# The state-space scan carried out inside the attention loop of a hybrid encoder layer

## The chip, the cores and the metric

The kernel runs on one core of a Trainium2 chip. The metric is the device time of one execution in microseconds (us), as the median of several runs. A profiled execution comes with its own time, with its span (from its first to its last instruction) and with the clock that was granted to TensorE.

## The reference, cut to what matters

One encoder layer on 1024 tokens of width 1024, all in float32:

```python
proj = x @ w_in                       # 512 columns u, 256 c_q, 128 + 32 ckv_rope
s = gelu(s5_bidirectional(u, ...))    # 32 groups of 16 channels, 64 complex states, two directions
s = s * sigmoid(s @ w_glu + b_glu)
a = mla(c_q, ckv_rope, ...)           # 8 heads, 1024 x 1024 scores each, softmax, times v
x1 = layer_norm(alpha * x + concat([s, a]) @ w_o)
out = layer_norm(alpha * x1 + moe(x1))  # 64 experts, top 6, one shared
```

`s5_bidirectional` runs, for each group and direction, the linear recurrence h[l] = a * h[l-1] + B u[l] over the 1024 tokens (backwards for the second direction) and reads it out as C h. `s` and `a` depend on `proj` alone and meet first in the product with `w_o`.

## The kernel before, in words

The stages stand one behind the other, each in a block of its own with a barrier at its end: `project` (projection, latents, coefficients of the scan), `attention`, `s5_scan`, `s5_gate`, `mix_norm_route`, `moe_experts`. Within a block each engine has its own list of instructions in a fixed order, written out by hand, and waits on counting semaphores for the others. `project` writes u to memory (`u_d`) and `s5_scan` reads it back from there; nothing of the scan depends on the attention.

`attention` (L480) loops over 8 heads, two to an iteration of the loop, and in a head over 8 tiles t of 128 queries. For a tile:

- TensorE multiplies queries by keys into `p_s` (`scores`, L529: two matmuls of 512 columns).
- VectorE takes the maximum of each row (`top`, L645) and scales it (L646). ScalarE takes the exponential into `pr` (L615), with the row's total beside it.
- TensorE transposes `pr` in eight blocks into `p_t` (L568). VectorE copies the first four blocks to `prT` (L659), ScalarE the last four (L620).
- TensorE multiplies `prT` by v into `p_o` (L582: eight matmuls). VectorE takes the reciprocal of the total (L650) and stores the scaled result (L651). These two are `finish`.

In the first seven tiles of a head TensorE also makes one of seven parts of the next head (`part`: two of q, L543; two of k, L546; two of turned q, L556; one of v, L550), which ScalarE copies out of the one bank `p_p` (`keep_part`). In tile 2 VectorE rotates the next head's q (`rotate`). `p_s`, `pr` and `prT` have two buffers each. In tile t TensorE's order is: wait for `pr` of tile t, transposes, scores of tile t + 2, the part, the product with v.

`s5_scan` (L684) works in 4 batches of 8 groups. For each of the two directions VectorE makes the matrices that bring the inputs of 8 tokens into the state (`combine` into `vs`, L867 to L869), the phases of the rotation (`tables`, L876 to L878), and the matrices that read the state out (`edges`: `ed1`, `ed2`). TensorE transposes `vs` (L766) and ScalarE copies the result to `w_in` (L807, L808). ScalarE makes sines and cosines of the phases (L811 to L814). TensorE multiplies `w_in` by the inputs U (`effects`, L752), and VectorE runs the recurrence on that (`run_states`, L847 to L859: rotate, scan, rotate back). TensorE also makes the short convolution within 8 tokens (L781). SyncE rearranges it from `ka` to `kt` by eight DMAs. At the end of a batch TensorE sums everything into `p_y` (L793 to L798), ScalarE copies it to `ysb` (L822), and SyncE stores it to `ys_d` by eight DMAs. U is loaded by eight DMAs at the start of the stage (L732). The eight PSUM banks are all in use, in either stage.

Of the kernel before, what the change touches and what calls it, by code (L numbers as in the profile page):

```python
# [13 lines left out]
P = 128  # L14
# [465 lines left out]
def attention(nc, k):  # L480
    SCALE = DQ ** -0.5
    with ExitStack() as ctx:
# [8 lines left out]
        bias = sb("bias", [P, 2], f32)  # L491
# [11 lines left out]
        scored, biased, probs, p_turned, pT_dve, pT_act = sem("scored"), sem("biased"), sem("probs"), sem("p_turned"), sem("pT_dve"), sem("pT_act")  # L503
        o_done, o_read, own = sem("o_done"), sem("o_read"), sem("own")
        PARTS = ("q", "q", "k", "k", "qT", "qT", "v")
        ROTATE = 2
        LINKS = 2 * T + 1
        block = ctx.enter_context(nc.Block())

        @block.sync  # L510
        def _(sp):
            def load(h, u):
                sp.dma_start(wq[:, u], k.w_uq[0].rearrange("(k p) n -> p k n", p=P)[:, :, bass.ds(h * DQ, DQ)]).then_inc(w_in[u], 16)
                sp.dma_start(wkv[:, u, :], k.w_ukv[0][:, bass.ds(h * (NOPE + DV), NOPE + DV)]).then_inc(w_in[u], 16)
            load(0, 0)
            load(1, 1)
            with sp.Fori(1, HEADS // 2) as hh:
                for u in range(2):
                    h = hh * 2 + u
                    sp.wait_ge(part_done, (h - 1) * len(PARTS))  # L520
                    load(h, u)

        @block.tensor
        def _(pe):
            def scores(h, u, t):
                if t == 0:
                    pe.wait_ge(part_kept, h * len(PARTS) + 6)
                for half in range(2):
                    last = nc.tensor.matmul(p_s[:, t % 2, half * 512:(half + 1) * 512], qT[:, u, t * P:(t + 1) * P],  # L529
# [3 lines left out]
            def part(h, u, i, nth_weights=None, first=False):  # L533
                what, second = PARTS[i], PARTS[:i].count(PARTS[i])
                if nth_weights is not None:
                    pe.wait_ge(w_in[u], nth_weights)
                if not first:
                    pe.wait_ge(part_kept, h * len(PARTS) + i)
# [19 lines left out]

            def head(hh, u, following):

                h = hh * 2 + u
                for t in range(T):
                    n = h * T + t
                    pe.wait_ge(probs, n + 1)
                    for half in range(2):
                        for r in range(4):
                            j = half * 4 + r
                            last = nc.tensor.transpose(p_t[:, j, :], pr[:, t % 2, j * P:(j + 1) * P], k.ident)  # L568
                        last.then_inc(p_turned, 1)
                    if t + 2 < T:  # L570
                        scores(h, u, t + 2)
                    elif following:
                        scores(h + 1, 1 - u, t + 2 - T)
                    if following and t < len(PARTS):
                        part(h + 1, 1 - u, t, (hh + u) * 32 + 32 if t == 0 else None)
                    pe.wait_ge(pT_dve, n + 1)
                    pe.wait_ge(pT_act, n + 1)
                    if t == 0:
                        pe.wait_ge(part_kept, h * len(PARTS) + 7)
                    pe.wait_ge(o_read, n + 1)  # L580
                    for j in range(T):
                        last = nc.tensor.matmul(p_o[:, 0:DV], prT[:, t % 2, j, :], v[:, u, j, :], start=(j == 0), stop=(j == T - 1))  # L582
                    last.then_inc(o_done, 1)

            for i in range(len(PARTS)):
                part(0, 0, i, 32 if i == 0 else None, first=(i == 0))
            scores(0, 0, 0)
            scores(0, 0, 1)
# [7 lines left out]
        def _(act):  # L596
            def keep_part(h, u, i):
                what, second = PARTS[i], PARTS[:i].count(PARTS[i])
                act.wait_ge(part_done, h * len(PARTS) + (i + 1))
# [6 lines left out]
                else:  # L606
                    last = nc.scalar.activation(qT[:, u, second * 512:(second + 1) * 512], p_p[0:DQ, :], ACT.Copy)
                last.then_inc(part_kept, 1)

            def head(hh, u, following):  # L610
                h = hh * 2 + u
                for t in range(T):
                    n = h * T + t
                    act.wait_ge(biased, n + 1)
                    nc.scalar.activation(pr[:, t % 2, :], p_s[:, t % 2, :], ACT.Exp, bias=bias[:, t % 2:t % 2 + 1], scale=SCALE,  # L615
                                         accum_out=total[:, t % 4:t % 4 + 1]).then_inc(probs, 1)
                    if following and t:
                        keep_part(h + 1, 1 - u, t - 1)
                    act.wait_ge(p_turned, 2 * n + 2)
                    nc.scalar.activation(prT[:, t % 2, 4:8, :], p_t[:, 4:8, :], ACT.Copy).then_inc(pT_act, 1)  # L620

            for i in range(len(PARTS)):
                keep_part(0, 0, i)
            with act.Fori(0, HEADS // 2 - 1) as hh:
# [6 lines left out]
        def _(dve):  # L631
            def rotate(ch, h):
                dve.wait_ge(part_kept, h * len(PARTS) + 2)
                q1, q2 = q[:, :, NOPE:NOPE + 16], q[:, :, NOPE + 16:DQ]
                nc.vector.tensor_tensor(rot[:, 0], q1, k.cos, ALU.mult)
                nc.vector.tensor_tensor(rot[:, 1], q2, k.sin, ALU.mult)
                nc.vector.tensor_tensor(rot[:, 2], q1, k.sin, ALU.mult)
                ch.link(nc.vector.tensor_tensor(rot[:, 3], q2, k.cos, ALU.mult))
                nc.vector.tensor_tensor(q1, rot[:, 0], rot[:, 1], ALU.subtract)
# [1217 lines left out]
```

## Time and profile before

| | |
|---|---|
| time, median of 3 runs | 1795.45 us (1794.26 to 1797.92) |
| time of the profiled execution | 1796.62 us |
| its span, granted clock | 1794.8 us, 0.927 |
| TensorE (PE) busy | 1566.9 us, 87% |
| VectorE (DVE) busy | 852.5 us, 47% |
| ScalarE (ACT) busy | 361.4 us, 20% |
| GpSimd (POOL) busy | 432.9 us, 24% |

Times of rows are in microseconds from the start of the span, those marked ns apart. PE is TensorE's matmuls and PEld its weight loads, which overlap them. A float32 matmul shows as two records. The granted clock is 1.00 at 2.4 GHz and 0.50 at 1.2 GHz. In a timeline the brackets at the end of a row give how long the engine was idle before it, and what ended that. "x8" says that eight instructions are merged in the row.

### The profile page before, as it was taken

To read this page: it belongs to the slowest core of one execution; us is meant where nothing else is said; L and a number is where in the kernel's file an instruction comes from. 1 tells how busy PE (TensorE), PEld (TensorE's weight loads), DVE (VectorE), ACT (ScalarE), POOL (GpSimd) and SP (SyncE) were. 2 spreads that over 40 slices of the span, in tenths; PEclk is the share of its full clock that TensorE was granted. 3 is DMA by queue.
4 is the path that set the end of the run, shared out by engine and by line. 5 is a ranking of instruction groups with operands and counts; after the bars stand their busy time and mean duration, and the time that the engine had idled before them with its cause. 6 is when DMAs were issued, how large, how long until landed. Compare 5 with 4: busy or idle time off the path is not lost. (4 is left out here: it accounts for less than half of the span.)

```text
span 1794.8 us, 18459 instructions
## 1 busy us (share of the span) xinstructions
PE 1566.9 (87%) x5878; PEld 894.7 (50%) x5878; DVE 852.5 (47%) x1618; ACT 361.4 (20%) x616; POOL 432.9 (24%) x444
## 2 busy tenths in 40 slices
PE   7989999999946565389999999999999999999990
PEld 4546777777735554235554444444444444444440
DVE  1462444444588888333886433333333333333335
ACT  1303443443433113111221001000000000000014
POOL 0000000000000000000244345555555555555530
PEclk9997999999967666689999999999999999999995
DMA  9010000000061101540005689999999999999956
GB/s 233 12 43 4 5 4 4 4 4 1 1 52 19 23 12 23 182 158 24 36 25 202 237 287 368 367 368 360 362 368 366 365 362 367 365 371 366 361 153 207
DMA packets 105149, 317.26 MB, mean 177 GB/s; under 512 B 38358, under 2 KB 55406, under 8 KB 80146
## 3 DMA queue, kind: packets, MB, share of 16 engines
q1 hardware_dynamic: 80546, 257.26, 39.1%
q0 software_dynamic: 23408, 59.45, 13.6%
q8 instruction: 23, 0.38, 0.1%
q10 hardware_dynamic: 1152, 0.00, 0.0%
q14 instruction: 20, 0.16, 0.0%
HBM read 271.73 MB, written 51.72 MB: 180 GB/s over the span
## 5 line engine op out<-in xcount | busy, mean ns | idle before, releaser
L1548 PE MATMUL moe_p_gu<-mixers_ring,moe_xgT 128*128 128x512 f32 x784 | 344.6, 592 | 0.0
L1679 DVE STREAM_TRANSPOSE moe_xgT<-moe_xg 128x1024 f32<-128x1024 f32 x65 | 132.1, 2032 | 417.7 <-DMA moe_xg<-x_d,moe_idx 417.7
L1494 POOL DMA_INDIRECT moe_xg<-x_d,moe_idx x260 | 263.6, 1014 | 116.1 <-issue 60.1
L1121 POOL DMA_INDIRECT slot_d<-all_entry,all_dest_i x48 | 48.0, 1001 | 928.4 <-DVE all_dest_i L1333 916.2
L1568 PE MATMUL moe_p_y<-mixers_ring,moe_hT 128*128 128x512 f32 x520 | 233.9, 592 | 0.9 <-DVE moe_hT L1690 0.9
L1548 PEld LDWEIGHTS moe_p_gu<-mixers_ring,moe_xgT 128*128 128x128 f32 x784 | 145.7, 191 | 164.5 <-issue 164.5
L1505 POOL DMA_INDIRECT sum_d<-moe_y,moe_idx x65 | 105.4, 1622 | 243.8 <-DMA sum_d<-moe_y,moe_idx 206.4
L1568 PEld LDWEIGHTS moe_p_y<-mixers_ring,moe_hT 128*128 128x128 f32 x520 | 98.7, 190 | 125.0 <-issue 123.9
L1616 ACT ACTIVATE moe_sig<-moe_p_gu 128x256 f32<-128x256 f32 x65 | 24.9, 383 | 582.0 <-PE moe_p_gu L1548 582.0
L582 PEld LDWEIGHTS att_p_o<-att_v,att_prT 128*128 128x128 f32 x1024 | 120.4, 192 | 19.5 <-issue 17.6
L582 PE MATMUL att_p_o<-att_v,att_prT 128*128 128x64 f32 x1024 | 123.7, 274 | 1.5 <-DVE att_prT L659 1.5
L529 PE MATMUL att_p_s<-latents_kT,att_qT 96*128 96x512 f32 x256 | 122.8, 603 | 0.0
L645 DVE TENSOR_REDUCE att_nmax<-att_p_s 128x1 f32<-128x1024 f32 x64 | 78.4, 1225 | 92.5 <-PE att_p_s L529 92.1
L1548 PE MATMUL moe_p_gu<-mixers_o,moe_xgT 128*128 128x512 f32 x256 | 113.9, 598 | 1.0
L752 PE MATMUL ssm_p_v<-ssm_U,ssm_w_in 128*128 x256 | 53.6, 399 | 46.6 <-DVE ssm_gsn L859 29.7
L752 PEld LDWEIGHTS ssm_p_v<-ssm_U,ssm_w_in 128*128 128x128 f32 x256 | 50.7, 305 | 50.8 <-DVE ssm_gsn L859 32.4
L1548 PEld LDWEIGHTS moe_p_gu<-mixers_o,moe_xgT 128*128 128x128 f32 x256 | 47.3, 190 | 57.2 <-issue 57.2
L615 ACT ACTIVATE att_pr<-att_p_s,att_bias 128x1024 f32<-128x1024 f32 x64 | 70.9, 1108 | 3.1 <-DVE att_bias L646 3.1
L568 PE MATMUL att_p_t<-all_const,att_pr 128*128 128x128 f32 x512 | 66.9, 274 | 0.4 <-ACT att_pr L615 0.4
L620 ACT ACTIVATE att_prT<-att_p_t 128x512 f32<-128x512 f32 x64 | 38.2, 597 | 138.6 <-PE att_p_t L568 138.6
L1622 ACT ACTIVATE moe_y<-moe_p_y,shared_block_w 128x512 f32<-128x512 f32 x65 | 44.7, 688 | 100.7 <-PE moe_p_y L1568 97.9
L1696 DVE TENSOR_SCALAR moe_y<-moe_p_y,shared_block_w 128x512 f32<-128x512 f32 x65 | 48.7, 750 | 29.8 <-PE moe_p_y L1568 26.0
(314 smaller groups left out, 1968.1 us busy)
## 6 DMA issues: line engine op xcount, KB each, us to landing
mixers_ring<-in_we_down_dram SPq DMA_DIRECT2D x65, 1024.0 KB
mixers_ring<-in_we_gate_dram SPq DMA_DIRECT2D x49, 1024.0 KB
mixers_ring<-in_we_up_dram SPq DMA_DIRECT2D x49, 1024.0 KB
mixers_o<-in_we_gate_dram SPq DMA_DIRECT2D x16, 1024.0 KB
mixers_o<-in_we_up_dram SPq DMA_DIRECT2D x16, 1024.0 KB
moe_xg<-x_d,moe_idx POOLq DMA_INDIRECT x260
all_x_sb<-in_x_dram SPq DMA_DIRECT2D x8, 512.0 KB, 11.7
mixers_ring<-in_w_o_dram SPq DMA_DIRECT2D x1, 4096.0 KB, 22.2
```

Of the source, the lines that this page charges most:

```text
L529: last = nc.tensor.matmul(p_s[:, t % 2, half * 512:(half + 1) * 512], qT[:, u, t * P:(t + 1) * P], kT[:, u, half * 512:(half + 1) * 512], ...
L568: last = nc.tensor.transpose(p_t[:, j, :], pr[:, t % 2, j * P:(j + 1) * P], k.ident)
L582: last = nc.tensor.matmul(p_o[:, 0:DV], prT[:, t % 2, j, :], v[:, u, j, :], start=(j == 0), stop=(j == T - 1))
L615: nc.scalar.activation(pr[:, t % 2, :], p_s[:, t % 2, :], ACT.Exp, bias=bias[:, t % 2:t % 2 + 1], scale=SCALE, accum_out=total[:, t % 4:t ...
L645: ch.link(nc.vector.tensor_reduce(nmax[:, t % 2:t % 2 + 1], p_s[:, t % 2, :], AX.X, ALU.max, negate=True))
L752: last = nc.tensor.matmul(p_v[:, x % 2, part, r, :], w_in[:, gd, part * N:part * N + P], U[:, bass.ds(b * GB + half * 4 + r, 1), :].rearra ...
L1494: nc.gpsimd.indirect_dma_start(xg[:, u, g, :], None, x1_quarters, bass.IndirectOffsetOnAxis(ap=idx[:, c, g:g + 1], axis=0), bounds_check=N ...
L1505: nc.gpsimd.indirect_dma_start(k.sum_d[:, :], bass.IndirectOffsetOnAxis(ap=idx[:, c, NQ:NQ + 1], axis=0), y[:, u, :], None, compute_op=ALU ...
L1548: last = nc.tensor.matmul(p_gu[:, u, :], xgT[:, u, kk, :], k.moe_gu[v][:, :, kk * F:(kk + 1) * F], start=(kk == 0), stop=(kk == KD - 1))
L1568: last = nc.tensor.matmul(p_y[:, half * 512:(half + 1) * 512], hT[:, u, kk, :], k.moe_dn[v][:, kk * D + half * 512:kk * D + (half + 1) * 512],
L1679: nc.vector.transpose(xgT[:, u].rearrange("p k (g i) -> p g k i", g=NQ), xg[:, u].rearrange("p g (j k) -> p g k j", k=KD)).then_inc(x_turn ...
L1696: nc.vector.tensor_scalar(y[:, u, 512:D], p_y[:, 512:D], k.block_w[:, bass.ds(col, 1)], None, ALU.mult).then_inc(y_dve, 1)
```

## The change

`attention` and `s5_scan` become one block, `attend_and_scan`. The scan now goes in 8 batches of 4 groups, one batch per head, and each of its pieces has a fixed place in one of the 8 tiles of a head:

- VectorE does a piece of the scan in tiles 0 to 6, behind its copy of `p_t` and ahead of `finish`. All its operations on a batch have half the elements that they had, and there are twice as many batches.
- TensorE's transposes of `vs`, its kernels and its outputs stand behind the product with v (tiles 1 and 2; 3 and 4; 7), its effects ahead of it (tiles 3 and 5). Transposes, kernels and outputs share the bank `p_p` with the parts of the next head.
- ScalarE keeps `vs` turned, makes the sines and cosines of both directions in tile 2 (one Abs and two Sin of 128 x 1024 for each head), and keeps kernels and outputs.
- To make room, `p_s`, `pr` and `prT` go from two buffers to one. The scores of tile t + 1 now stand at the start of tile t, ahead of the transposes. ScalarE's exponential of tile t + 1 now stands behind its copy of `p_t` and behind `keep_part` of tile t.
- The scaling of the row maximum (L646) is gone: the scale goes into the copy of the turned q.
- U is loaded at the start of the combined block, and TensorE waits for it before the first head. The transfers of `kt` and `ys_d` stand in SyncE's list behind the loads of the weights of the head after next.
- The turned probabilities are copied half by VectorE, half by ScalarE, as before.

The core of the diff (bodies that only moved are left out; in round brackets what stands there unchanged):

```diff
-def attention(nc, k):
+def attend_and_scan(nc, k):
...
-        pr = sb("pr", [P, 2, SEQ], f32)
-        prT = sb("prT", [P, 2, T, P], f32)
-        p_s = ps("p_s", [P, 2, SEQ])
+        pr = sb("pr", [P, SEQ], f32)
+        prT = sb("prT", [P, T, P], f32)
+        p_s = ps("p_s", [P, SEQ])
+        p_v = ps("p_v", [P, 2, GB, NC])
+        quarters = p_p[:, :].rearrange("p (r n) -> p r n", r=GB)
...
# TensorE, head(): order within tile t
                     pe.wait_ge(probs, n + 1)
+                    if t + 1 < T:
+                        scores(h, u, t + 1)
+                    elif following:
+                        scores(h + 1, 1 - u, 0)
                     (eight transposes of pr into p_t)
-                    if t + 2 < T:
-                        scores(h, u, t + 2)
...
                         part(h + 1, 1 - u, t)
+                    if t == 3:
+                        effects(h, 0)
+                    if t == 5:
+                        effects(h, 1)
                     pe.wait_ge(pT_dve, n + 1)
                     pe.wait_ge(pT_act, n + 1)
...
                     (eight matmuls into p_o)
+                    if t in (1, 2):
+                        turn_vs(h, t - 1)
+                    if t in (3, 4):
+                        kernels(h, 4 - t)
+                    if t == 7:
+                        outputs(h)
...
+            pe.wait_ge(u_in, 16 * T)      # ahead of the first head
# ScalarE, head()
+                    act.wait_ge(p_turned, 2 * n + 2)
+                    nc.scalar.activation(prT[:, 4:8, :], p_t[:, 4:8, :], ACT.Copy).then_inc(pT_act, 1)
+                    if following and t < NP:
+                        keep_part(h + 1, 1 - u, t)
+                    if following or t + 1 < T:
+                        exponent(n + 1, (t + 1) % T)
+                    if t in (1, 2):
+                        keep_vsT(h, t - 1)
+                    if t == 2:
+                        turn_phases(h)          # Abs, Sin, Sin, each 128 x 1024
+                    if t in (3, 4):
+                        keep_kernels(h, 4 - t)
+                    if t == 7:
+                        keep_outputs(h)
# VectorE, head()
+                    if following or t + 1 < T:
+                        top(h * T + (t + 1), (t + 1) % T)
+                    dve.wait_ge(p_turned, (h * T + t) * 2 + 1)
+                    nc.vector.tensor_copy(prT[:, 0:4, :], p_t[:, 0:4, :]).then_inc(pT_dve, 1)
+                    if t == 0:
+                        inputs(chs, h, 0)
+                        phases(chs, h, 0)
+                    if t == 1:
+                        inputs(chs, h, 1)
+                        phases(chs, h, 1)
+                    if t == ROTATE:
+                        edge(chs, h, 1)
+                        if following:
+                            rotate(ch, h + 1)
+                    if t == 3:
+                        edge(chs, h, 0)
+                        other_edge(chs, h, 1)
+                    if t == 4:
+                        states(chs, h, 0)
+                    if t == 5:
+                        add_kernels(h)
+                        other_edge(chs, h, 0)
+                    if t == 6:
+                        states(chs, h, 1)
+                    finish(ch, h, t)
# SyncE, per head
+                sp.wait_ge(ka_done, b + 1)
+                (eight loads of kt from ka)
+                sp.wait_ge(y_kept, b + 2)
+                (eight stores of ysb to ys_d)
...
-                    attention(nc, k)
-                s5_scan(nc, k)
+                    attend_and_scan(nc, k)
```

The new functions of the scan have the same operations as before, on 4 groups instead of 8. `inputs` is one `combine` (three operations of 128 x 512), `phases` three operations of 128 x 512, `edge` a copy and a `combine` (three of 128 x 576), `other_edge` a `combine`, `states` is `run_states`, and `add_kernels` one small addition (its copy of 16 x 448 goes to ScalarE).

## Rows read from the trace of the kernel before

**Rows 1.** Stretches: PE, PEld, DVE, ACT, POOL busy (instructions), clock, DMA share, GB/s.

```profile
159.80:497.00 337.20, 334.99 (x2204) 258.79 (x2204) 163.55 (x360) 137.60 (x241) 0.00 (x0) 1.00 0.01 3
...
497.00:741.00 244.00, 134.66 (x768) 120.51 (x768) 195.64 (x268) 58.07 (x80) 0.00 (x0) 0.68 0.23 26
```

**Rows 2.** Stretches: one head, one batch of scan, one tile of the last head.

```profile
164.20:207.50 43.30, 43.30 (x287) 33.32 (x285) 20.69 (x46) 17.48 (x31) 0.00 (x0) 1.00 0.02 5
...
549.90:607.20 57.30, 33.80 (x194) 30.15 (x193) 48.87 (x66) 14.46 (x20) 0.00 (x0) 0.68 0.13 19
...
488.90:492.50 3.60, 2.87 (x26) 2.66 (x26) 1.10 (x3) 1.69 (x3) 0.00 (x0) 1.00 0.00 0
```

**Rows 3.** Timeline, what opens tiles 1 to 4: start, us, engine, line.

```profile
165.96 1.04 PE L568 MATMUL att_p_t<-all_const,att_pr 128*128 128x128 f32 x8
...
172.08 1.04 PE L568 MATMUL att_p_t<-all_const,att_pr 128*128 128x128 f32 x8
...
177.61 1.04 PE L568 MATMUL att_p_t<-all_const,att_pr 128*128 128x128 f32 x8
...
183.14 1.04 PE L568 MATMUL att_p_t<-all_const,att_pr 128*128 128x128 f32 x8
```

**Rows 4.** Timeline of one tile of the last head, which has no part.

```profile
484.59 1.04 PE L568 MATMUL att_p_t<-all_const,att_pr 128*128 128x128 f32 x8
...
484.79 0.16 DVE L650 RECIPROCAL att_rtotal<-att_total 128x1 f32<-128x1 f32 x1 [0.32 <-PE att_p_o L582]
...
485.24 0.69 DVE L659 COPY att_prT<-att_p_t 128x512 f32<-128x512 f32 x1
...
485.47 1.88 PE L529 MATMUL att_p_s<-latents_kT,att_qT 96*128 96x512 f32 x4
...
485.67 0.60 ACT L620 ACTIVATE att_prT<-att_p_t 128x512 f32<-128x512 f32 x1 [2.64 <-PE att_p_t L568]
...
486.17 1.11 ACT L615 ACTIVATE att_pr<-att_p_s,att_bias 128x1024 f32<-128x1024 f32 x1
...
487.19 1.90 PE L582 MATMUL att_p_o<-att_v,att_prT 128*128 128x64 f32 x16
...
487.39 1.23 DVE L645 TENSOR_REDUCE att_nmax<-att_p_s 128x1 f32<-128x1024 f32 x1 [1.47 <-PE att_p_s L529]
...
488.92 1.05 PE L568 MATMUL att_p_t<-all_const,att_pr 128*128 128x128 f32 x8
```

**Rows 5.** Timeline of VectorE's scan, and matmuls that it releases.

```profile
585.38 0.69 DVE L847 TENSOR_TENSOR ssm_ta<-ssm_p_v,ssm_tc 128x512 f32<-128x512 f32 x1
...
587.52 1.37 DVE L855 TENSOR_TENSOR_SCAN ssm_tb<-states_m,ssm_ta 128x128 f32<-128x128 f32 x4
...
590.28 3.78 PE L752 MATMUL ssm_p_v<-ssm_U,ssm_w_in 128*128 x16 [5.16 <-DVE ssm_gsn L859]
...
607.25 1.23 DVE L867 TENSOR_TENSOR ssm_ta<-states_pb,states_b 128x1024 f32 x1 [0.64 <-DVE ssm_gsn L859]
```

**Rows 6.** Timeline, first and last of five output matmuls at clock 1.00.

```profile
733.00 0.39 PE L793 MATMUL ssm_p_y<-ssm_U,ssm_kt 128*128 x2
...
733.90 0.39 PE L798 MATMUL ssm_p_y<-ssm_gsn,ssm_ed 128*128 128x128 f32 x2
```

**Rows 7.** Timeline of ScalarE, a table load and the sine behind it.

```profile
510.43 1.28 ACT L812 ACT_TABLE_LOAD   x1
...
511.73 1.15 ACT L812 ACTIVATE ssm_ts<-ssm_fr,all_const 128x1024 f32<-128x1024 f32 x1
```

**Rows 8.** Timeline, load of U, its first reader, end of the scan stage.

```profile
497.14 10.56 SPq L732 DMA_DIRECT2D ssm_U<-u_d  x8
...
522.22 6.02 PE L752 MATMUL ssm_p_v<-ssm_U,ssm_w_in 128*128 x32 [13.66 <-DMA ssm_U<-u_d]
...
734.32 0.60 ACT L822 ACTIVATE ssm_ysb<-ssm_p_y 128x512 f32<-128x512 f32 x1 [3.81 <-PE ssm_p_y L798]
...
741.03 0.38 SPq L934 DMA_DIRECT2D mixers_ring<-ys_d  x1
```

More of the change, by code:

```diff
@@ L613, in head @@
                     n = h * T + t
[L614 to L618, printed above, removed]
-                    act.wait_ge(p_turned, 2 * n + 2)
-                    nc.scalar.activation(prT[:, t % 2, 4:8, :], p_t[:, 4:8, :], ACT.Copy).then_inc(pT_act, 1)
-            for i in range(len(PARTS)):
+                    act.wait_ge(p_turned, 2 * n + 2)
+                    nc.scalar.activation(prT[:, 4:8, :], p_t[:, 4:8, :], ACT.Copy).then_inc(pT_act, 1)
+                    if following and t < NP:
+                        keep_part(h + 1, 1 - u, t)
[9 more added lines that the diff above has]
+                        keep_outputs(h)
+            act.sem_inc(y_kept, 1)
+            for i in range(NP):
                 keep_part(0, 0, i)
+            exponent(0, 0)
             with act.Fori(0, HEADS // 2 - 1) as hh:
@@ L650, in finish @@
                 ch.link(nc.vector.reciprocal(rtotal[:, t % 2:t % 2 + 1], total[:, t % 4:t % 4 + 1]))
-                nc.vector.tensor_scalar(k.o[:, t, bass.ds(h * DV, DV)], p_o[:, 0:DV], rtotal[:, t % 2:t % 2 + 1], None,
-                                        ALU.mult).then_inc(o_read, 1)
-            def head(hh, u, following):
-                h = hh * 2 + u
-                ch = Chain(dve, own, h * LINKS + 3)
-                for t in range(T):
-                    dve.wait_ge(p_turned, (h * T + t) * 2 + 1)
-                    nc.vector.tensor_copy(prT[:, t % 2, 0:4, :], p_t[:, 0:4, :]).then_inc(pT_dve, 1)
-                    if t + 2 < T:
-                        top(ch, h, t + 2)
-                    elif following:
-                        top(ch, h + 1, t + 2 - T)
-                    finish(ch, h, t)
-                    if following and t == ROTATE:
-                        rotate(ch, h + 1)
-                assert ch.n == LINKS or not following
@@ new lines, in states @@
+            def states(ch, b, d):
+                own_rows = slice(d * GB, (d + 1) * GB)
+                if d == 0:
+                    dve.wait_ge(tab_done, b + 1)
+                dve.wait_ge(v_done, b * 2 + d + 1)
+                tt(ra, p_v[:, 0], cos_t[:, own_rows, :], ALU.mult)
+                ch.link(tt(rb, p_v[:, 1], sin_t[:, own_rows, :], ALU.mult))
+                dve.sem_inc(v_read, 1)
+                ch.link(tt(ra, ra, rb, ALU.add))
+                for r in range(GB):
+                    decay = k.m8[:, bass.ds(b * GB + d * G + r, 1)].to_broadcast([P, NC])
@@ new lines, in _ @@
+            for g in (gc, gsn):
+                nc.vector.memset(g[:, 0:GB, 0:1], 0.0)
+                nc.vector.memset(g[:, GB:NG, NC:NC + 1], 0.0)
+            dve.sem_inc(o_read, 1)
+            dve.sem_inc(v_read, 1)
+            rotate(Chain(dve, own), 0)
+            top(0, 0)
+            with dve.Fori(0, HEADS // 2 - 1) as hh:
+                for u in range(2):
+                    head(hh, u, True)
+            head(HEADS // 2 - 1, 0, True)
+            head(HEADS // 2 - 1, 1, False)
```

444 lines of the change are left out of this document (198 added, 246 removed).

## The prediction

> **What bounds the kernel now.** I read the stretches by stage first. The attention takes 337 us, and TensorE is busy for all but about 2 of them, at clock 1.00. The scan behind it takes 244 us, in which TensorE is busy 135 us at a mean clock of 0.68, VectorE 196 us and ScalarE 58 us [rows 1]. Then I read one period of each. A head is 43.3 us long with TensorE busy 43.3, VectorE 20.7 and ScalarE 17.5. A batch of the scan (8 groups) is about 57.5 us long with VectorE busy 48.9 [rows 2]. So the attention is bound by TensorE, the scan by VectorE's work and the handoffs around it, and each leaves free the engine that the other wants. What follows at 741 us is the gate, the mixing and the experts. The change touches nothing of it, so I carry its 1054 us over unchanged.
>
> **What goes.** The stage from 497 to 741 us goes as a stage. Its last copy on ScalarE starts at 734.3 and the next stage at 741.0 [rows 8]; that tail (final store, its wait, the barrier) stays, now behind the combined loop. Taken from the end of TensorE's last output, 734.1, it is 6.9 us. The load of U goes off the path: its eight DMAs are issued from 497.1, and the first reader starts at 522.2, 25.1 us later [rows 8]. It will now be issued behind the first weights, from about 131.8 us, and land at about 157, while TensorE makes the parts of head 0 and the softmax of its first tile. The first head opens at 159.8 [rows 1]. The margin is 3 us, and each us beyond it costs one us, once.
>
> **What TensorE must do for a head.** Without a part a tile is 4.33 us (484.59 to 488.92): transposes 0.88, scores 1.72, product with v 1.73 [rows 4]. With a part of q it is 6.12 and with one of k 5.53 [rows 3]. A part of turned q is four transposes more, at the 0.11 of the other eight, so 4.77, and the part of v has as many records as one of q, 1.8. A head is 8 x 4.33 + 2 x 1.79 + 2 x 1.20 + 2 x 0.44 + 1.8 = 43.3, as measured. To this the change adds matmuls of 128 columns, which follow each other at 0.22 us ((733.90 - 733.00) / 4, [rows 6]): eight effects twice (1.78 each), four kernels twice (0.89 each), 20 outputs (4.45). And it adds four transposes twice (0.44 each). In all 10.7, so a head is 54.0 us of TensorE. By tile: 6.12, 6.56, 5.97, 8.20, 5.66, 6.55, 6.13, 8.78.
>
> **What VectorE must do for a head.** An operation of 128 x 512 takes 0.69 (0.61 to 0.72 from start to start), one of 128 x 1024 1.23. Halving one does not halve its time [rows 5]. One `states` on 4 groups is what L847 to L859 are now: 585.38 to 590.28, 4.9 us [rows 5]. From these: `inputs` 2.3, `phases` 2.15, `edge` 2.5, `other_edge` 2.1, and `add_kernels` 0.3. The pieces by tile are 4.45, 4.45, 3.9 (with `rotate`), 4.7, 4.9, 2.4, 4.9 and 0: 29.7 us. The attention's own share of a tile is top 1.25, copy 0.68 and finish 0.5 [rows 4], 19.4 for eight. So 49.1 us against TensorE's 54.0: both are nearly full, and neither can wait long for the other.
>
> **What ends last in each tile.** With one `p_s` and one `pr` there is a closed ring. A tile opens when the exponential of its scores is there; then scores of the next (ready 1.92 after the opening: 485.47 to 487.39, [rows 4]), top (1.25), exponential (1.2: 1.11 and the read of the total), and 0.06 to hand over. That makes 4.4 us, less than any tile of TensorE. But the exponential now stands behind `keep_part`, top behind VectorE's piece of the tile before, and the product with v behind VectorE's copy. Going through the eight tiles with these durations (a is the opening of the tile, both engines running on from tile to tile):
> - Tile 0: the part of q is ready at a + 4.6, kept at 5.1, exponential until 6.3: 6.35 instead of 6.12.
> - Tile 1: VectorE is free at a + 2.45, top until 3.7, copy until 4.4, just as TensorE wants it: 6.61 (+0.05).
> - Tile 2: VectorE is free at a + 2.7, copy until 4.65, where TensorE is ready at 3.8: 6.88 (+0.91).
> - Tile 3: ScalarE has kept the second `vs` and has Abs, a table load (1.28) and two Sin (1.15 each) [rows 7] until a + 5.8. Its copy of `p_t` ends at 6.4, its exponential, with a second table load ahead of it, at 9.5: 9.56 instead of 8.20 (+1.36).
> - Tile 4: the short part leaves TensorE waiting for the copy until a + 3.9: 6.53 (+0.87).
> - Tile 5: `states` ends at a + 2.7, the effects cover it: 6.55.
> - Tile 6: as tile 0, with v: 6.46 (+0.33).
> - Tile 7: `states` again until a + 2.9, copy until 4.8, where TensorE was ready at 2.6: 10.96 (+2.18).
>
> The sum is 59.9 us a head, 5.9 of it waits. The last head has no parts to make but all of the scan. There VectorE is late in nearly every tile, and the same steps give 58.1. Seven heads and the last: 477.4 us.
>
> **What no row shows.** TensorE gets about three more waits in each tile. A tile with a part of k takes 1.20 more, where its two passes of 512 columns should take 0.86 (half of the scores' 1.72) [rows 3, 4], so a small instruction behind a wait can cost up to 0.3. The bounds are 0 and 0.3 us for each of 64 tiles, 0 to 19 us. I take 0.1, 6 us, because nearly all waits stand ahead of long series with work queued in front of them. The eight `kt` DMAs and the eight stores of `ys_d` I cost at nothing: the `kt` data are ordered in tile 5 and wanted at the end of tile 7, more than 15 us later, and the stores have a whole head; that cover would have to shrink to about 9 us before it cost anything. The dropped L646 shortens a path that no longer ends last.
>
> **The sum.** 159.8 + 477.4 + 6 + 6.9 = 650.1, where the stage behind began at 741.0: 90.9 us less. From the profiled execution's own 1796.6 that is 1705.7. Its median lies 1.2 lower, so 1704.5 us.
>
> On the table loads the trace and the Trainium skill differ. The load at 510.43 takes 1.28 us and the sine behind it starts 0.02 us after its end [rows 7]. The page "ScalarE: Activation LUTs", section "What ACT_TABLE_LOAD costs", puts another 1.38 us of drain on each switch. By the page two switches in tile 3 would add 2.8 us a head, 22 us in all, and the time would be an estimated 1727. The row decides here.
>
> **Rivals.**
> 1. VectorE sets the pace. If its scan pieces take a quarter longer than summed (37 instead of 29.7 us a head), as chains of short operations with a semaphore each may, tiles 1, 2, 5 and 7 each wait 1.1 to 1.2 us more. A head becomes 64.5, the loop 514 + 6, the time 1741. For it: it has 49 us of work in a head of 60, all in one fixed order, and in tiles 2, 4 and 7 TensorE already waits for it. Against it: the 4.9 us of `states` are measured with their links.
> 2. The overlap is perfect: TensorE's 54.0 us a head and 45.3 in the last, and nothing on top. The loop is 423, the time 1645. For it: a steady head now has no gap at all. Against it: that was with two buffers.
> 3. The clock falls, and the kernel is slower than before. In the scan stage, where TensorE was busy 55% of the time and stood still for 5 us at a time before a group of matmuls, its mean clock was 0.68 [rows 1, 5]. If the gaps of the new loop bring it there, 54.0 / 0.68 + 5.9 = 85 us a head, the loop is 682 and the time 1795.5 + 109 = 1904. It decides from a head of 71.8 us on ((741.0 - 159.8 - 6.9) / 8), a mean clock of 0.82. Against it: the last tiles of the attention have TensorE waiting in every tile (2.87 busy of 3.60) and kept 1.00 [rows 2], and my gaps are at most 2.2 us in a loop busy nine tenths. The Trainium skill, "TensorE: Matmul & The Clock Gate", section "HAM oscillation", tells of a kernel that lost the clock in every wait between its tiles; by that rule the scan stage above behaves as the page says, the last tiles of the attention show waits that are too short for it.
> 4. The scan is moved, but little of it is hidden, because the shared bank `p_p` strings the engines together: each of its nine handoffs a head (matmuls, copy, next matmuls) shows as a wait of the 0.58 to 1 us that such turns cost in the scan stage. That is up to 8 us a head, 68 us, the time about 1769.
>
> **How the numbers follow.** Chances: forecast 0.58 (its own range, 1685 to 1725, from 0 to 19 us of waits and a few us either way on the pieces), rival 1 0.17, rival 2 and what lies between it and the forecast 0.10, rival 4 0.10, rival 3 0.05. The range 1665 to 1745 takes in rival 1, half of the way to rival 2, and leaves out rivals 3 and 4. About 0.2% (3.6 us) is what a measurement can tell from no change. Only rival 3 is slower, and a mix of 3 and 4 could land at no change: faster 0.94, same 0.01, slower 0.05.
>
> **What would show it.** In the new profile the distance between the opening scores of two heads should be 59 to 62 us with a granted clock near 1.00, TensorE about 90% and VectorE about 80% busy. Tile 3 and tile 7 should be the longest; the idle time of L582's successor should be put down to the copies of `p_t`, and TensorE's idle time at the start of a tile to the exponential, largest behind a table load. The stage behind should start at about 650 us and look as before. A head above 64 us, a clock under 0.95 in the loop, or waits for `kt` or U would prove a step wrong.

## The result, and the profile after

The changed kernel takes 1714.28 us (median of 4 runs, 1707.58 to 1719.85), the kernel before 1796.18 (1794.26 to 1797.92). The ratio is 0.9543, with a 95% interval of 0.9507 to 0.9579: faster by 82 us. The forecast was 1704.5, its own range 1685 to 1725. The profiled execution took 1714.97 us.

The page of the profile after, first lines of its first part (busy us and share of the span):

```profile
span 1713.1 us, 18584 instructions
PE 1554.4 (91%) x5878; PEld 880.9 (51%) x5878; DVE 842.6 (49%) x1650; ACT 373.1 (22%) x638; POOL 432.9 (25%) x444
```

The busy time of every engine is within 13 us of what it was. But for the small scaling of the maximum no work has gone; it now stands beside other work. The stretches of the new loop, of everything behind it, of head 5 (an undisturbed head), of tile 7 in heads 2 and 5, and of tile 0 in heads 0 and 4 (columns as in [rows 1]):

```profile
158.65:653.05 494.40, 460.32 (x2976) 366.89 (x2976) 349.99 (x657) 206.81 (x342) 0.00 (x0) 0.95 0.05 11
659.17:1713.10 1053.93, 957.33 (x2464) 437.41 (x2464) 436.46 (x832) 137.68 (x230) 432.69 (x440) 0.96 0.80 282
472.63:531.48 58.85, 55.97 (x382) 44.30 (x381) 44.00 (x83) 26.50 (x44) 0.00 (x0) 1.00 0.06 13
335.08:349.35 14.27, 12.47 (x69) 11.23 (x69) 4.83 (x11) 1.80 (x3) 0.00 (x0) 0.76 0.00 0
520.47:531.48 11.01, 9.21 (x68) 7.97 (x69) 4.83 (x11) 1.80 (x3) 0.00 (x0) 1.00 0.01 1
158.65:167.03 8.38, 8.38 (x44) 6.16 (x44) 4.40 (x6) 2.18 (x4) 0.00 (x0) 0.75 0.01 2
410.40:418.34 7.94, 7.94 (x44) 6.75 (x44) 5.51 (x8) 2.18 (x4) 0.00 (x0) 0.79 0.25 54
```

Where 337 and 244 us stood [rows 1], there are 494. The stage behind starts at 659.17 instead of 741.03 [rows 8] and takes the same 1054 us as before; the whole gain, 81.9 us, is made in this loop. The fourth and the fifth line show the same tile 7, the same busy VectorE and the same instructions, once in 14.27 us at a mean clock of 0.76 and once in 11.01 at 1.00.

The timeline of tile 7 in head 1 (start, us, engine, line), up to the opening of head 2:

```profile
272.60 1.04 PE L653 MATMUL att_p_t<-all_const,att_pr 128*128 128x128 f32 x8
...
273.58 1.21 DVE L806 TENSOR_REDUCE att_nmax<-att_p_s 128x1 f32<-128x1024 f32 x1
...
274.71 0.68 DVE L882 COPY att_prT<-att_p_t 128x512 f32<-128x512 f32 x1
...
275.44 3.60 PE L678 MATMUL att_p_o<-att_v,att_prT 128*128 128x64 f32 x16 [1.80 <-DVE att_prT L882]
...
280.23 0.63 PE L633 MATMUL att_p_p<-att_gc,att_ed 128*128 128x128 f32 x2
...
283.04 0.39 PE L633 MATMUL att_p_p<-att_gc,att_ed 128*128 128x128 f32 x2
...
287.15 1.98 PE L577 MATMUL att_p_s<-latents_kT,att_qT 96*128 96x512 f32 x4 [1.94 <-issue]
```

Read it from the brackets. TensorE has transposed, and waits 1.80 us for VectorE's copy, which stands behind the maximum of 1.21. The product with v then takes 3.60 us where it takes 2.00 in head 5, and a pair of output records 0.63 instead of 0.39: half clock, 1.2 GHz, until about 282, and then 2.4 again. Ahead of head 2 TensorE stands for 1.94 us with nothing that it waits for: there the hardware loop over pairs of heads turns. The waits of the loop by releaser (us in total, times, longest; the two lines of "issue" are waits for which the profile names no releaser):

```profile
PE att_p_o L678 <- DVE att_prT L882: 25.3, 20, 3.0
...
PE att_p_o L678 <- issue: 4.0, 8, 1.6
PE att_p_s L577 <- issue: 4.0, 2, 2.0
```

No wait of any weight for `kt`, for U, for the effects or for the bank `p_p` is among them.

### The profile page after: what moved, and what is told of

It reads as the page before. It is cut to its first block and busy times, and to the rows that moved or that the text cites. A ratio compares the mean times of both kernels' runs of the same rounds, so it can differ in the third digit from the quotient of the medians.

```text
span 1713.1 us, 18584 instructions
## 1 busy us (share of the span) xinstructions
PE 1554.4 (91%) x5878; PEld 880.9 (51%) x5878; DVE 842.6 (49%) x1650; ACT 373.1 (22%) x638; POOL 432.9 (25%) x444
## 5 line engine op out<-in xcount | busy, mean ns | idle before, releaser
L678 PE MATMUL att_p_o<-att_v,att_prT 128*128 128x64 f32 x1024 | 130.4, 283 | 29.6 <-DVE att_prT L882 25.3
L678 PEld LDWEIGHTS att_p_o<-att_v,att_prT 128*128 128x128 f32 x1024 | 124.0, 198 | 41.9 <-DVE att_prT L882 36.6
L577 PE MATMUL att_p_s<-latents_kT,att_qT 96*128 96x512 f32 x256 | 129.1, 628 | 7.0 <-issue 4.0
L653 PEld LDWEIGHTS att_p_t<-all_const,att_pr 128*128 128x128 f32 x512 | 61.3, 143 | 34.0 <-issue 34.0
L729 ACT ACTIVATE att_pr<-att_p_s,att_nmax 128x1024 f32<-128x1024 f32 x64 | 70.9, 1108 | 6.9 <-DVE att_nmax L806 6.8
L577 PEld LDWEIGHTS att_p_s<-latents_kT,att_qT 96*128 96x128 f32 x256 | 45.1, 196 | 46.5 <-issue 39.8
## 6 DMA issues: line engine op xcount, KB each, us to landing
mixers_o<-in_we_up_dram SPq DMA_DIRECT2D x16, 1024.0 KB, 15.6
```

Of the source, the lines that this page charges most:

```text
L577: last = nc.tensor.matmul(p_s[:, half * 512:(half + 1) * 512], qT[:, u, t * P:(t + 1) * P], kT[:, u, half * 512:(half + 1) * 512], start=T ...
L653: last = nc.tensor.transpose(p_t[:, j, :], pr[:, j * P:(j + 1) * P], k.ident)
L678: last = nc.tensor.matmul(p_o[:, 0:DV], prT[:, j, :], v[:, u, j, :], start=(j == 0), stop=(j == T - 1))
L729: nc.scalar.activation(pr[:, :], p_s[:, :], ACT.Exp, bias=nmax[:, t % 2:t % 2 + 1], accum_out=total[:, t % 4:t % 4 + 1]).then_inc(probs, 1)
```

## The experiments

Each was timed beside the kernel before, whose median lay between 1796.8 and 1797.4 us. A gain against the change is the difference to its 1714.28 us; each timeline and stretch is of one profiled execution. Everything behind the loop took 1054 to 1059 us in these executions, so a few us between two medians cannot be laid to the loop. The theory after the result: the work and its overlap are as forecast, and the 10 us missing come from TensorE's waits costing more than their length, since the clock falls behind them. The rivals: the loop's turn, ScalarE's long list in tile 3, and a VectorE that is late through the scan.

**e1_outputs_first.** In tile 7 the outputs of the scan go ahead of the product with v, into the wait.

```diff
+                    if t == 7:
+                        pe.wait_ge(part_kept, kept + NP)
+                        outputs(h)
                     pe.wait_ge(pT_dve, n + 1)
                     ...eight matmuls into p_o...
-                    if t == 7:
-                        outputs(h)
```

> In tile 7 the 20 output matmuls stand ahead of the product with v instead of behind it. Theory (TensorE's wait for VectorE's late copy in tile 7, 1.8 us, also costs it the clock): the wait and the slow stretch both go, 1.9 us a head and about 20 us of half-clock time over the loop, so the loop shrinks from 494 to about 462 us, time about 1682 us, and tile 7 is about 9 us in every head. Rival A (the slow stretch comes from the output matmuls' own short form, not from the wait): only the waits go, 15 us, time about 1699, and half-clock records stay among the outputs. Rival B (the clock has nothing to do with tile 7): the same 15 us.

Measured: 1685.59 us (1679.36 to 1686.02), ratio 0.9367 [0.9352, 0.9382], 28.7 us better than the change. The product with v no longer waits in tile 7 of heads 0 to 6, and the tile is 8.9 us (9.05 in heads 1 and 3, without the turn of the loop behind it), with the product and the outputs at full speed. Rows of the profile, stretches of head 0's tile 7 with what stands around it, and of the tile behind a turn of the loop:

```profile
207.10:217.70 10.60, 10.52 (x83) 9.38 (x83) 5.87 (x12) 4.02 (x7) 0.00 (x0) 1.00 0.02 4
276.77:286.01 9.24, 9.23 (x45) 7.02 (x45) 5.18 (x8) 2.19 (x4) 0.00 (x0) 0.67 0.18 41
```

And its timeline at that turn:

```profile
272.80 1.90 PE L684 MATMUL att_p_o<-att_v,att_prT 128*128 128x64 f32 x16
276.77 2.07 PE L577 MATMUL att_p_s<-latents_kT,att_qT 96*128 96x512 f32 x2 [2.08 <-issue]
```

Against the undisturbed 11.01 us a tile this is 2.1 less, 17 us in 8 heads; about 12 more are time that the half clock no longer takes (an estimate, the rest of the gain). What is left is plain too: 2.08 us of standing still at the turn, and a tile 0 of 9.24 at a clock of 0.67, where head 5 of the change has 6.19; in head 4 it is 9.44 us behind 2.30.

**e2_fill_wait.** Nothing is moved; eight matmuls whose result nobody reads fill the wait of tile 7.

```diff
+                    if t == 7:
+                        pe.wait_ge(part_kept, kept + NP)
+                        for r in range(8):
+                            nc.tensor.matmul(quarters[:, r % GB, :], k.ident, U[:, r, :],
+                                             start=True, stop=True)
                     pe.wait_ge(pT_dve, n + 1)
```

> Eight extra matmuls of 128 columns (1.8 us, results unused) run in tile 7 where TensorE waits for VectorE's copy; the order is otherwise unchanged. Theory: TensorE is no longer idle ahead of the product with v, the clock stays at 1.00, product and outputs run at full speed; tile 7 is about 11.0 us in every head instead of 11.0 to 14.3, the time falls by 14 to 20 us to about 1697 although TensorE does more. Rival (the clock falls for another reason): the time stays at 1713 or rises.

Measured: 1700.86 us (1695.03 to 1711.46), 0.9465 [0.9438, 0.9493], 13.4 better, with ranges that overlap, and with more work for TensorE. Stretches, tile 7 of head 0, and the last head:

```profile
208.21:219.23 11.02, 11.00 (x85) 9.80 (x85) 4.84 (x11) 1.80 (x3) 0.00 (x0) 1.00 0.01 1
577.80:646.18 68.38, 60.62 (x334) 47.23 (x332) 41.74 (x76) 21.80 (x35) 0.00 (x0) 0.80 0.04 8
```

The tile is as long as the undisturbed one (11.01), and now it is so in each of heads 0 to 6 (10.90 to 11.18 us, clock 1.00). This tells the clock from the wait: the work that fills the wait does nothing but keep the engine busy, and the up to 3.4 us of half clock go. The last head takes 68.38 us at a mean clock of 0.80 in this execution, 7.1 more than in the change, and gives back over half of what tile 7 gained: the whole loop is 487.9 us instead of 494.4. This execution was the slowest of the five, and fillers in tile 7 alone don't keep the clock everywhere.

**e3_phases_in_tile_3.** ScalarE's Abs, two Sin and their table loads go from tile 2 to tile 3, behind the exponential that TensorE waits for.

```diff
-                    if t == 2:
+                    if t == 3:
                         turn_phases(h)
```

> Abs, Sin, Sin and their table load stand in ScalarE's list in tile 3 behind the exponential, instead of in tile 2. Theory (ScalarE's table work delays its copy of p_t in tile 3): TensorE's product with v in tile 3 no longer waits 0.4 us and its next opening no longer waits for the exponential, tile 3 falls from 9.05 to about 8.3 us, minus 0.7 us a head, time 1706 to 1709. Rival: it only moves the lateness to tile 4, where copy and table load meet, and the time stays at 1713 or rises by up to 8 us.

Measured: 1707.52 us (1701.98 to 1713.07), 0.9503 [0.9484, 0.9522], 6.8 better, with ranges that overlap. Tile 3 goes from 9.05 to 8.39 us in heads 0 to 6 and from 8.98 to 7.19 in the last, 6.4 us in all, and no other tile of an undisturbed head changes. ScalarE's list cost this much. The loop of this execution is 16.1 us shorter (478.2), the rest for half clock that did not come: tile 7 waits 1.7 to 1.8 us in heads 0 to 6 as before, yet only two of these tiles are slow (12.65 us, heads 0 and 4) where the change had five. The edit does not touch tile 7, so how often the clock falls behind the same wait is not fixed.

**e4_unrolled.** The loop over pairs of heads is written out for TensorE, ScalarE and VectorE.

```diff
-            with pe.Fori(0, HEADS // 2 - 1) as hh:
+            for hh in range(HEADS // 2 - 1):
                 for u in range(2):
                     head(hh, u, True)
```

> The loops over pairs of heads on TensorE, ScalarE and VectorE are written out. Theory (the gaps of 1.94 and 2.05 us ahead of the opening scores of heads 2 and 4 are the turn of the loop): they go, time minus 4 us, about 1710. Rival (longer code has to be fetched and costs as much): no change.

Measured: 1700.8 us (1698.44 to 1703.74), 0.9464 [0.9451, 0.9477], 13.5 better. The two gaps of 2 us are gone, an undisturbed head is 58.65, and tile 7 is still 14.15, 14.15 and 12.52 us in heads 0, 1 and 4. The gaps account for 4.0 of the 13.5, the 0.2 us by which a head in the loop is shorter for 1.2; the rest are stretches at half clock that did not come. One kind of them goes with the turn: over the change, e1, e2, e3, e7 and e8, the tile 0 behind such a gap was slow (7.94 to 9.44 us) after 7 of 12 turns, and it never was in heads 2 and 4 of e4, e5 and e9, which have no turn. For tile 7, slow three times here and five times in the change, nothing shows that it hung on a gap; e3 has two with both gaps in place.

**e5_three_edits.** e1, e3 and e4 together.

> The three edits together: outputs ahead of the product in tile 7, ScalarE's table work in tile 3, loops written out. Theory (TensorE's waits, and the half-clock stretches that follow the two longest of them, are what separates a head from its work): no wait of TensorE's above 0.6 us is left and no slow stretch, every head is 56.1 us, the loop about 446 us, time about 1665 us. Rival (the clock falls now and then whatever the waits): half-clock stretches remain and the time is 1680 or more.

Measured: 1673.5 us (1671.74 to 1677.6), 0.9315 [0.9299, 0.9331]. The edits gain 40.8 where their sum was 49.0, as two of them remove stretches of the same kind (an explanation that no run tests). The loop is 447.5 us, as expected (446), and behind its opening no wait above 0.6 us is left in heads 0 to 6. The time is 8.5 us above the 1665 expected all the same; everything behind the loop took 1058.1 us here, 4.2 more than in the change. Two stretches of lower clock are left, tile 0 of head 0 (8.73 us at 0.71) and tile 1 of the last head (7.48 at 0.77). One head in the stretches:

```profile
442.66:498.71 56.05, 55.41 (x383) 44.19 (x382) 44.18 (x83) 26.62 (x44) 0.00 (x0) 1.00 0.06 13
```

**e6_one_after_the_other.** The rest of the change without its overlap: single buffers, batches of 4 groups and ScalarE's order as in the change, but the scan's pieces taken out of the tiles and run behind the attention, batch by batch, within the same block.

```diff
-                    if t == 3:
-                        effects(h, 0)
...and so with all other pieces, on three engines
             head(HEADS // 2 - 1, 1, False)
+            with pe.Fori(0, HEADS) as b:
+                scan(b)          # turn_vs, effects, kernels, outputs
```

> The changed kernel with the overlap undone: the same attention loop (one p_s, one pr, exponential behind keep_part, no scaling of the maximum) without the scan's pieces, then the same pieces of the scan batch by batch (8 batches of 4 groups). Theory (the gain is the overlap, and everything else in the change costs time): the attention loop is about 354 us instead of 334 before, the scan 265 to 295 us instead of 237, time about 1856 us (1840 to 1870), slower than the kernel before by some 60 us. Rival (a good part of the gain is the dropped scaling, the new batches or the new order): at or below 1796 us.

Measured: 1833.79 us (1833.65 to 1837.83), 1.0208 [1.0193, 1.0224], slower than before by 37, where 60 were expected (1840 to 1870 us). Stretches: its attention, its scan, a head, a batch:

```profile
158.73:545.00 386.27, 361.66 (x2208) 269.77 (x2208) 153.16 (x298) 134.55 (x240) 0.00 (x0) 0.97 0.01 3
545.00:776.97 231.97, 119.65 (x768) 107.19 (x768) 204.35 (x361) 71.95 (x103) 0.00 (x0) 0.80 0.09 18
255.96:303.44 47.48, 45.08 (x287) 33.95 (x286) 19.46 (x38) 17.26 (x31) 0.00 (x0) 1.00 0.01 4
716.82:744.14 27.32, 14.86 (x97) 13.33 (x98) 25.53 (x46) 9.15 (x14) 0.00 (x0) 0.81 0.10 19
```

So the overlap is worth 1833.8 - 1714.3 = 120 us, and the change without it costs 37. The single buffers, with the order of scores and exponential that goes with them, make a head 47.48 us instead of 43.30 [rows 2], and the attention 386 instead of 337; which of the two costs what was not told apart. The scan in half batches is not longer: 232 us instead of 244, of which 13.7 were TensorE's wait for U [rows 8], and two batches of 4 groups take 54.6 where one of 8 took 57.3 [rows 2]. VectorE is busy 204 us in it instead of 196 [rows 1]; halving the operations made its work 4% dearer. The same hardware loop over pairs of heads turns here without a gap, as in the kernel before; its body is shorter by the pieces of the scan. Tile 0 is slow in heads 4 and 5 all the same (9.59 us at 0.64, 7.94 at 0.79), with no wait above 1.04 us in these heads.

**e7_no_vector_pieces.** VectorE's pieces of the scan are left out, but for the short sum of the kernels; only their signals are sent. The scan's outputs are not computed.

```diff
-                    if t == 4:
-                        states(chs, h, 0)
+                    if t in (4, 6):
+                        dve.wait_ge(v_done, h * 2 + t // 2 - 1)
+                        dve.sem_inc(v_read, 1)
+                        dve.sem_inc(g_done, 1)
...and so with inputs, phases, edge and other_edge
```

> VectorE's pieces of the scan are left out (it only signals; matrices and states are zeros), TensorE and ScalarE do all that they did. Theory (VectorE's lateness makes the waits of tile 7 and of the last head, and through them the clock): tile 7 is about 8.8 us, tile 4 about 6.2, no slow stretch, a head 56.5 us, time about 1690 us. Rival 1 of the forecast (VectorE sets the pace of the whole head): a head falls to its 54 us of TensorE work, time 1650 or less. Other rival (VectorE is not what is waited for): 1713 us.

Measured: 1697.95 us (1690.55 to 1701.62), 0.9432 [0.9411, 0.9453]. The stretch of an undisturbed head:

```profile
459.52:517.62 58.10, 55.98 (x383) 44.29 (x381) 19.58 (x39) 26.41 (x44) 0.00 (x0) 1.00 0.06 13
```

VectorE does 19.6 us a head instead of 44.0, and the head is shorter by 0.75. Half clock still came, once in tile 7 (head 4, 11.87 us instead of 10.25, behind a wait of 1.04) and in the last head, whose tile 4 ran all at 0.50. The stretch of that tile:

```profile
604.21:615.83 11.62, 10.89 (x37) 7.44 (x36) 2.27 (x4) 2.28 (x4) 0.00 (x0) 0.50 0.00 0
```

VectorE's timeline in tile 7 of head 5:

```profile
509.39 1.23 DVE L806 TENSOR_REDUCE att_nmax<-att_p_s 128x1 f32<-128x1024 f32 x1 [1.46 <-PE att_p_s L577]
...
510.53 0.68 DVE L882 COPY att_prT<-att_p_t 128x512 f32<-128x512 f32 x1
...
511.26 2.00 PE L678 MATMUL att_p_o<-att_v,att_prT 128*128 128x64 f32 x16 [1.04 <-DVE att_prT L882]
```

With none of the scan but the short sum on VectorE, TensorE still waits 1.04 of its 1.80 us, and tile 4 is 6.81 as before (6.2 was expected). In what is left the copy (0.68) stands behind the maximum (1.23) in VectorE's list, which e8 tests. Taking the scan away is worth 0.76 us of wait a head.

**e8_copy_first.** VectorE's copy of `p_t` goes ahead of the row maximum.

```diff
-                        top(h * T + (t + 1), (t + 1) % T)
                     dve.wait_ge(p_turned, (h * T + t) * 2 + 1)
                     nc.vector.tensor_copy(prT[:, 0:4, :], p_t[:, 0:4, :]).then_inc(pT_dve, 1)
+                    if following or t + 1 < T:
+                        top(h * T + (t + 1), (t + 1) % T)
```

> The changed kernel with one edit: VectorE copies its half of p_t before it takes the maximum of the next tile's scores, instead of after it. Theory (what TensorE waits for in tiles 4 and 7 is the 1.25 us maximum that stands ahead of the copy in VectorE's list, far more than the scan piece of the tile before): tile 4 falls from 6.8 to 6.2 us, tile 7 from 11.0 to 9.9 without a slow stretch, a head from 58.9 to about 57.1, time 1682 to 1690 us. Rival (the maximum, now 0.7 us later, delays the exponential and with it the opening of every tile): gains in tiles 4 and 7 are given back in tiles 0, 1, 2 and 6, time 1705 to 1715 us.

Measured: 1698.72 us (1698.56 to 1699.48), 0.9452 [0.9439, 0.9464], 15.6 better and not the 24 to 32 expected. An undisturbed head is 57.71, with tile 7 at 10.31 and tile 4 at 6.47. Its timeline in tile 7:

```profile
507.84 0.28 DVE L811 TENSOR_SCALAR mixers_o<-att_p_o,att_rtotal 128x64 f32 x1
508.04 0.68 DVE L880 COPY att_prT<-att_p_t 128x512 f32<-128x512 f32 x1
508.64 1.22 DVE L806 TENSOR_REDUCE att_nmax<-att_p_s 128x1 f32<-128x1024 f32 x1
508.78 2.00 PE L678 MATMUL att_p_o<-att_v,att_prT 128*128 128x64 f32 x16 [1.10 <-DVE att_prT L880]
```

The copy can't start before `states` and `finish` have ended at 508.04, so 1.10 of the 1.80 us stay. With e7 this says that the two causes overlap: the order alone gives back 0.70, the scan alone 0.76, and each leaves a wait that the other makes. In heads 0, 2 and 4 half clock still followed that shorter wait (tile 7 at 11.96). The loop is 475.0 us, 19.4 less than in the change; everything behind it took 4.9 more here.

**e9_four_edits.** e5 and e8 together, the best version.

> That edit on top of the three together (outputs ahead of the product, table work in tile 3, loops written out). Theory: tile 4 falls by 0.6 us, tile 7 has no wait left to lose, tiles without a part in the last head fall from 5.7 to about 5.5: a head 55.5 us, time 1673.5 minus 6, about 1667 us. Rival (the later maximum costs as much): 1672 to 1680 us.

Measured: 1669.51 us (1667.57 to 1673.13), 0.9286 [0.9273, 0.9299]: 127.9 us below the kernel before and 44.8 below the change. Against e5 the ranges overlap, and the loop is only 0.8 us shorter (446.8): tile 4 falls by 0.26 and tile 2 by 0.10, tile 7 rises by 0.20. Its stretch of a head:

```profile
441.74:497.62 55.88, 55.58 (x383) 44.22 (x382) 44.18 (x83) 26.75 (x44) 0.00 (x0) 1.00 0.06 13
```

And what TensorE still waits for VectorE in the whole loop, 4.1 us instead of 25.3:

```profile
PE att_p_o L684 <- DVE att_prT L882: 4.1, 5, 0.9
```

TensorE is busy 55.58 of a head's 55.88 us; a shorter head would have to take work from it.

## Why the prediction was right, and where it missed

**What goes, and what is carried over.** Right. The stage behind measured 1053.9 us, the tail 6.1 (6.9 forecast), the first head opened at 158.65 (159.8). U's loads were issued at 130.90, and what opened the first head was the exponential (an idle time of 2.55 behind L729), not U.

**TensorE's work.** 54.0 us a head forecast, 55.97 busy measured in head 5. The excess is 0.1 in each of tiles 0 to 2 and 5 (6.19, 6.66 and 6.07 us in the first three, from 6.12, 6.56 and 5.97), and 0.3 to 0.6 in tiles 3, 4, 6 and 7. The openings of tiles 2 to 4 and of tile 7 in head 5 (timeline), to be read against [rows 3]:

```profile
485.48 1.88 PE L577 MATMUL att_p_s<-latents_kT,att_qT 96*128 96x512 f32 x4
...
491.55 1.88 PE L577 MATMUL att_p_s<-latents_kT,att_qT 96*128 96x512 f32 x4
...
500.60 1.98 PE L577 MATMUL att_p_s<-latents_kT,att_qT 96*128 96x512 f32 x4
...
504.50 2.00 PE L678 MATMUL att_p_o<-att_v,att_prT 128*128 128x64 f32 x16 [0.60 <-DVE att_prT L882]
...
520.47 1.98 PE L577 MATMUL att_p_s<-latents_kT,att_qT 96*128 96x512 f32 x4
...
525.13 2.00 PE L678 MATMUL att_p_o<-att_v,att_prT 128*128 128x64 f32 x16 [1.80 <-DVE att_prT L882]
```

**VectorE's work.** 49.1 us forecast, 44.0 busy measured. The two are not the same measure: the forecast goes from start to start, the busy time leaves out the short gaps between dependent operations. From start to start the pieces of head 5 take 4.14, 4.06, 3.81, 4.52, 4.96, 2.1 and 4.98 us, 28.6 in all where I summed 29.7, so the sum was good to 4%. `states` of tile 4 goes from the first of these rows to the second, 4.96 us where the row said 4.9:

```profile
504.37 0.68 DVE L854 TENSOR_TENSOR att_ta<-att_p_v,att_tc 128x512 f32<-128x512 f32 x1
...
509.33 0.17 DVE L810 RECIPROCAL att_rtotal<-att_total 128x1 f32<-128x1 f32 x1
```

The difference lies in tiles 0 and 1 (4.45 forecast for each). With it VectorE was free 1.9 us after tile 2 had opened, not 2.7, its copy ended at 3.7, not 4.65, and the wait forecast there (+0.91) did not come: the tile measured 6.07.

**What ends last in each tile.** The sum was 59.9 us and an undisturbed head is 58.85: 2.0 more of work, 3.0 less of waits (2.9, not 5.9). Forecast and measured by tile: 6.35 and 6.19, 6.61 and 6.66, 6.88 and 6.07, 9.56 and 9.05, 6.53 and 6.81, 6.55 and 6.65, 6.46 and 6.41, 10.96 and 11.01. Tiles 3 and 7 are the longest, as said. The reason given for tile 7, `states` in front of the copy, was half of it: without the scan 0.76 of the 1.80 us go (e7), without the maximum ahead of the copy 0.70 (e8).

**The step that failed** is the one headed "What no row shows", the 6 us for waits, together with the sentence under rival 3 that gaps of at most 2.2 us in a loop busy nine tenths would leave the clock at 1.00. The mechanism and the sign of the forecast were right, and this term of the sum was mis-sized. The row set against rival 3 could not carry that sentence: the last tiles of the attention that kept 1.00 had waits of 0.73 us each (the two tiles from 488.92 on; the one before, in [rows 4], has none), not of 2. The term measured 26.1 us, of two parts:

- 22.1 us of half clock. Tile 7 took 14.26, 14.42, 14.27, 11.16, 12.64, 11.01 and 12.52 us in heads 0 to 6, without the turns of the loop: 13.2 over the undisturbed 11.01 each. Head 7 was 61.29 at a mean clock of 0.92. Its tiles 0 to 5 took 41.90, where e4 took 40.24 at full clock, and in its tile 7 the product and the first 12 outputs ran at half clock, 3.3 us more than at full: 56.3 and 5.0 of half clock (an estimate). Tile 0 took 8.38 and 7.94 in heads 0 and 4 instead of 6.2: 3.9. e2 shows the cause in tile 7: the wait filled, the tile is 10.9 to 11.2 us at a clock of 1.00 in heads 0 to 6. Over all runs tile 7 was slow in 14 of 35 such heads with a wait in it, and in none of 28 without.
- 4.0 us for two turns of the hardware loop (1.94 and 2.05), which my sum had nowhere. e4 shows it.

The whole: 7 x 58.85 + 56.3 = 468.3 instead of 477.4, then 22.1 + 4.0 instead of 6. That is 494.4 us instead of 483.4, and with the opening (-1.15) and the tail (-0.8) the stage behind starts 9.1 us later than forecast, 659.2 instead of 650.1. That the time came within 10 us is in part luck: 9 us too much for the heads were set against 20 too little for what no row showed. And one sign of a wrong step that the forecast had named did come: heads 0 and 1 took 64.3 and 64.2 us, above its 64, and the loop's clock was at its 0.95.

Three small slips of the forecast change nothing: rival 3 is 108 us above the kernel before by its own terms, not 109; rival 4's 8 us a head are 64, not 68, which is what its 1769 goes by; and the two pieces of tile 3 add up to 4.6, not 4.7.

**The rivals.** Rival 1 (VectorE sets the pace) is refuted by e7: with more than half of VectorE's work gone a head gets 0.75 us shorter. Rival 2 (perfect overlap) did not come with this order of work, but e9 comes within 25 us of its 1645, and a head within 1.9 of its 54.0. Rival 3 named the right mechanism, and the case against it was what failed: a mean clock of 0.95 in the loop, where it needed 0.82 to turn the sign. Rival 4 (the shared bank) left no wait behind: of 494.4 us TensorE was busy 460.3, and 25.3 of the other 34.1 were waits for one copy of VectorE's.

**The two rules.** The table loads behave as the row of before said. ScalarE's timeline of tile 3, head 0:

```profile
181.80 1.28 ACT L751 ACT_TABLE_LOAD   x1
...
183.10 1.15 ACT L751 ACTIVATE att_ts<-att_ts,all_const 128x1024 f32<-128x1024 f32 x1
...
186.26 1.28 ACT L729 ACT_TABLE_LOAD   x1
...
187.56 1.11 ACT L729 ACTIVATE att_pr<-att_p_s,att_nmax 128x1024 f32<-128x1024 f32 x1
```

Each next operation starts 0.02 us behind the load's end. The drain that the Trainium skill adds ("ScalarE: Activation LUTs", "What ACT_TABLE_LOAD costs") is not to be seen here; the measurement decides, and tile 3 is 9.05 us. On the clock I had weighed the section "HAM oscillation" of the page "TensorE: Matmul & The Clock Gate" of the Trainium skill and found my waits too short. The trace showed half clock behind 1.80 us. The next section of that page of the Trainium skill, "A second HAM failure mode: psum-queue depth-cycling", tells of a kernel in which frequent small pauses between groups of matmuls made the clock swing. It names no length of a pause; that short ones can be enough is what this trace agrees with (1.80 us, and 1.04 in e7), and it is the case that I should have weighed.

## What to carry to other kernels

Moving work of another engine under a full TensorE paid 120 us here although the change without the overlap cost 37; when such a change is sized, take the waits of TensorE that it leaves and allow for a stretch at half clock behind the long ones (here 1.5 to 3.4 us behind about half of those of 1.8), not for their length alone. Then look at what independent matmuls stand behind the longest wait: moved ahead of it, they were worth 28.7 us, where these waits were 15.5. An engine that is late is not always one with too much work: ask first whether the one small operation that others wait for stands behind a longer one in its own list (e8: 15.6 us for one swap).

## What the runs showed of the hardware

- Behind waits of 1.80 us, in a loop in which TensorE is busy 93% of the time, the clock fell to 1.2 GHz in five of the seven heads 0 to 6, and cost 1.5 to 3.4 us each time. Over the change, e3 and e4, with waits of 1.7 to 1.8 us in tile 7 of heads 0 to 6, it fell in 10 of 21 such tiles, and with waits of 1.0 to 1.1 us (e7, e8) in 4 of 14. Where the wait was filled or moved (e1, e2, e5, e9) the product and the outputs of that tile kept 2.4 GHz in all 28. It did not fall behind each wait: head 5 had the same 1.80 and stayed at 2.4 GHz. What decides between them was not found.
- TensorE stands still for 1.5 to 2.3 us where a hardware loop of two heads turns, with no wait for another engine (12 turns in six runs); the tile behind ran at a clock of 0.66 to 0.79 after 7 of them (0.67 and 0.66 in e1) and at 1.00 after 5. Where the loop's body is shorter (the kernel before and e6: 287 matmul records a head instead of 382) the turn shows no gap.
- The change's runs lie 12.3 us apart, those of the kernel before 3.7. That the stretches at half clock make the time vary is likely but not shown: the runs of e4 and e9 lie 5.3 and 5.6 apart, those of e2 16.4, but those of e8 only 0.9, with three slow tiles 7 in its profiled execution.
